# Rotary half-swap by VectorE's shuffle in place of products with a constant matrix

## The reference

```
parts = split(h @ w_in)                     # ten blocks of 1024 columns: b, c, xin, za, q, k, v, zb, ga, gb
q = apply_rope(heads(parts[4]), cos, sin)   # 16 heads of 64
k = apply_rope(heads(parts[5]), cos, sin)
v = heads(parts[6])
attn = neighbourhood_attention(q, k, v, k_ctx, v_ctx, rpb)
y = mixer_out(parts, attn, ...)

def rot_half_axial(u):                      # over the 64 features of a head
    u1, u2, u3, u4 = split(u, 4)            # four groups of 16
    return concatenate([-u2, u1, -u4, u3])
def apply_rope(u, cos, sin):
    return u * cos + rot_half_axial(u) * sin
```

## Time and profile before

| | us |
|---|---|
| median of 3 runs | 1343.25 |
| lowest and highest run | 1339.63, 1343.4 |
| profiled execution, its own time | 1342.57 |
| span of the profiled execution | 1340.4 |

### The profile page before, as it was taken

The page is one execution under the profiler, slowest core; times in us unless marked ns, Lnnn a source line. Parts: engine busy times, 40 slices in busy tenths (PEclk is TensorE's granted clock), DMA queues, the critical chain, the costliest instruction groups (busy, mean ns, idle before and its releaser), DMA issues.

```text
span 1340.4 us, 14669 instructions
## 1 busy us (share of the span) xinstructions
PE 1237.3 (92%) x6021; PEld 858.2 (64%) x6021; DVE 302.1 (23%) x652; ACT 207.4 (15%) x419; POOL 107.1 (8%) x117
## 2 busy tenths in 40 slices
PE   4999899999999989898989889889999999999997
PEld 4887788887853434434343324378888888876686
DVE  2035213543130111101110111121001004426511
ACT  1222452220110000000000000110000000025501
POOL 0015002510100000000000000000000000025300
PEclk9999899999989898898979898998999999999999
DMA  8879323333649999999999999952444444344300
GB/s 286 265 249 321 123 97 123 125 127 102 252 188 401 376 418 409 417 409 419 417 393 418 418 419 413 377 185 94 157 149 147 146 155 157 126 157 124 97 0 32
DMA packets 149737, 324.57 MB, mean 242 GB/s; under 512 B 8655, under 2 KB 111546, under 8 KB 133178
## 3 DMA queue, kind: packets, MB, share of 16 engines
q1 hardware_dynamic: 143818, 315.39, 63.0%
q0 software_dynamic: 1536, 4.20, 1.1%
q10 hardware_dynamic: 4336, 4.30, 1.0%
HBM read 321.77 MB, written 1.05 MB: 241 GB/s over the span
## 4 chain that ended last, share of the span: by engine, by line
PE 77%; DMA 8%; issue 7%; DVE 4%; ACT 2%; SPq 1%; POOL 1%; DVEq 0%; POOLq 0%; ACTq 0%
PE bank L551 31%; PE bank L817 14%; PE bank L554 13%; DMA ring<-in_w 7%; PE bank L837 5%; PE bank L794 3%; DVE X L1732 1%; PE bank L854 1%; PE bank L711 1%; PE bank L909 1%; DMA ring<-in_w_in 1%; PE bank L605 1%; PE bank L942 1%; PE bank L922 1%; ACT AR L1147 1%
## 5 line engine op out<-in xcount | busy, mean ns | idle before, releaser
L551 PE MATMUL bank<-HT,ring 128*128 128x256 f32 x1856 | 409.1, 382 | 4.3 <-DVE HT L1403 3.7
L551 PEld LDWEIGHTS bank<-HT,ring 128*128 128x128 f32 x1856 | 354.8, 192 | 56.4 <-DVE HT L1403 4.4
L817 PE MATMUL bank<-ring,AR 128*64 128x512 f32 x640 | 169.1, 593 | 3.9 <-DMA ring<-in_w 3.9
L554 PE MATMUL bank<-ring,HT 128*128 128x256 f32 (+1 forms) x576 | 129.1, 385 | 8.1 <-DMA ring<-in_w_in 6.9
L817 PEld LDWEIGHTS bank<-ring,AR 128*64 128x64 f32 x640 | 56.4, 137 | 112.9 <-issue 112.9
L554 PEld LDWEIGHTS bank<-ring,HT 128*128 128x128 f32 x576 | 110.3, 196 | 24.6 <-issue 8.2
L817 PE MATMUL bank<-AR 128*64 128x512 f32 x384 | 125.0, 663 | 0.1
L837 PE MATMUL bank<-ring,AR 128*64 128x512 f32 x384 | 87.7, 598 | 11.4 <-ACT AR L1147 11.4
L554 PE MATMUL bank<-ring,AR 128*128 128x256 f32 x328 | 74.5, 390 | 4.4 <-DVE AR L1850 1.5
L1720 DVE TENSOR_TENSOR AR<-AR,bank 128x256 f32<-128x256 f32 x32 | 13.5, 421 | 286.1 <-ACT AR L1140 286.1
L1267 POOL TENSOR_TENSOR SM<-SM 128x2 f32<-128x2 f32 (+3 forms) x9 | 12.3, 1368 | 787.7 <-DVE SM L1383 727.5
(11 more groups left out here) (307 smaller groups left out, 912.2 us busy)
## 6 DMA issues: line engine op xcount, KB each, us to landing
ring<-in_w SPq DMA_DIRECT2D x128, 1024.0 KB, 15.4
ring<-in_w_in SPq DMA_DIRECT2D x67, 1024.0 KB, 5.1
AR<-in_w SPq DMA_DIRECT2D x64, 1024.0 KB, 11.4
ring<-in_w_mod SPq DMA_DIRECT2D x12, 1024.0 KB, 6.0
ring<-in_w_out SPq DMA_DIRECT2D x4, 1024.0 KB, 6.0
ring<-in_w_ple_gate SPq DMA_DIRECT2D x4, 1024.0 KB, 9.7
ring<-in_w_out_conv SPq DMA_DIRECT2D x4, 1024.0 KB, 5.1
AR<-in_bias POOLq DMA_DIRECT2D x32, 128.0 KB, 2.4
```

What stands on the lines that cost most here:

```text
L551: mm = pe.matmul(bank[:, part * T:part * T + T], w[:, k, c0 + part * P:c0 + part * P + P], act[:, k, :], start=(k == 0), stop=(k == k_n - 1))
L554: mm = pe.matmul(bank[:, part * 256:part * 256 + n], act[:, k, part * P:part * P + P], w[:, k, c0:c0 + n], start=(k == 0), stop=(k == k_n ...
L817: mm = pe.matmul(bank[e * SLOT:e * SLOT + SLOT, :].rearrange("p (w n) -> p w n", w=2), XG[:, k, :], w, start=(k == 0), stop=(k == DK - 1))
```

## The change

The swap of the two groups of 16 partitions is done by one instruction of VectorE, `stream_shuffle`, which lets each partition of a group of 32 take the data of another of the same group. It reads `RAW` and writes into the destination of the rotated result. The minus sign of the rotation, which a shuffle can't give, is put into the table of sines. The multiplication by the sine table now reads and writes the destination in SBUF and no longer reads a PSUM bank. TensorE's eight products with `rot` fall away with their waits, and `rot` itself, 128 of the columns of `CST`. VectorE waits for ScalarE's copy in place of TensorE's product.

```
-            def rotate(m):
-                i = (of["q2"] + of["k2"])[m]
-                pe.wait_ge(S("emptied_act"), emptied[i][1])
-                if m >= 2:
-                    pe.wait_ge(S("roped"), m - 1)
-                pe.matmul(B[4 + m % 2][:, :], const("rot"), RAW[:, m % 2, :], start=True, stop=True)\
-                  .then_inc(S("rot_ps"), 1)
-            for m, i in enumerate(of["q2"] + of["k2"]):
-                product(i, HT)
-                if m:
-                    rotate(m - 1)
-            product(of["v2"][0], HT)
-            rotate(7)
-            for i in of["v2"][1:]:
-                product(i, HT)
+            products("q2", HT)
+            products("k2", HT)
+            products("v2", HT)
             pe.wait_ge(S("roped"), 8)
...
-                dve.wait_ge(S("rot_ps"), m + 1)
+                dve.wait_ge(S("emptied_act"), emptied[i][1])
                 d3 = dst.rearrange("p (a t) -> p a t", a=2)
-                V_.tensor_tensor(d3, B[4 + m % 2][:, :].rearrange("p (a t) -> p a t", a=2),
-                                 over(const("sinT").unsqueeze(1), 2, T), ALU.mult)
+                link(V_.stream_shuffle(dst, RAW[:, m % 2, :], [(lane + 16) % 32 for lane in range(32)]))
+                V_.tensor_tensor(d3, d3, over(const("sinT").unsqueeze(1), 2, T), ALU.mult)
...
-    put("sinT", np.sin(ang.astype(np.float64)))
+    put("sinT", np.sin(ang.astype(np.float64)) * np.where(i % 32 < 16, -1.0, 1.0)[:, None])
```

More of the change, by code:

```diff
@@ L60 @@
 CONST_COLS, _at = {}, 0
-for _name, _n in (("ident", 128), ("ustrict", 128), ("ones", 256), ("rot", 128), ("cosT", 256), ("sinT", 256),
+for _name, _n in (("ident", 128), ("ustrict", 128), ("ones", 256), ("cosT", 256), ("sinT", 256),
                   ("winmask", 256), ("invfreq", 16), ("iota_slot", 128), ("rev8", 8), ("pick2", 2), ("row0", 128), ("round_id", ROUNDS)):
@@ L79, in constants @@
     put("ones", 1.0)
[L81 to L87, removed]
     half = HD // 2
```

## The result

| | before | after |
|---|---|---|
| median, 14 runs each (us) | 1339.61 | 1331.34 |
| lowest and highest (us) | 1334.73, 1343.4 | 1323.78, 1335.54 |
| profiled execution (us) | 1342.57 | 1323.78 |
| its span (us) | 1340.4 | 1321.6 |

The ratio is 0.9929, with a 95% interval from 0.9907 to 0.9951: 9.5 us faster, between 6.6 and 12.5. It isn't the ratio of the two medians, which lie 8.3 us apart. One later execution of the kernel before took 3628.36 us, in the slow state, and is left out of every figure here. The kernel before came out at 1339.61 us over 14 runs; the three that the prediction had seen had a median of 1343.25.

A forecast was written before the change was run, and what follows sets the result against it. TensorE, busy without a gap in the queries and keys, was taken as the bound. Rotations (6.87 us) and shorter constant tile (0.2) sum to 7.07 us off the median 1343.25, giving 1336.2 us; range 1331.5 to 1340.

The forecast's parts named there:

- The place and the mechanism: Stage of queries and keys: eight rotations of 0.86 us are links of TensorE's chain; removing them takes off 6.87 us.
- The hidden work: VectorE, queries and keys: eight shuffles of 0.69 us, 5.8 us together with their waits, cost the path nothing.
- cover of a turn: VectorE, queries and keys: with the shuffle added, about 2 us stay idle in each turn of a 6.91 us product.
- The limit: Before the scores: each shuffle may take 5.7 us before TensorE waits for a rotated result.
- the banks' limit: Queries, keys and values: a product waits for the copy four products back, called looser than the limit of the scores.
- The constant tile: Start of the kernel: 64 KB less to load brings the first fill and product forward by 0.2 us, bounds 0 and 0.3.
- The biases' lead: GpSimd's first three biases, about 20 us ahead of the last copy of values, gain some 10 us on that lead.
- the last step of the sum: Whole kernel: 7.07 us taken off the median of 1343.25 us gives 1336.2 us.
- rival B: After the changed stage, perhaps at the scores: the gain is given back, 1343.1 us if all, 1339.7 if half; chance 0.12.

## Why the prediction was right or wrong

**The place and the mechanism held.** The rotations were links of the chain, and their removal shortened the stage by 6.86 us where 6.87 was forecast. Doubling them cost 6.87; VectorE's part without TensorE's gave nothing.

**The hidden work was hidden.** A shuffle takes 0.72 us where 0.69 was taken, plus the forecast gap and the short load of the permutation: 8 x 0.76 = 6.1 us of VectorE time in place of 5.8. The prediction's cover of a turn was right as well: 1.85 us of waiting behind a turn of queries, 2.30 behind one of keys. The rule of the Trainium skill, "VectorE: DVE Perf Modes", "The perf-mode tier table", that the shuffle has no faster program, agrees with the trace: 0.72 us is near the 0.69 of a one-pass row and far from 0.43. The eight took 5.8 us without their gaps, against the 5.5 that the prediction worked out by that rule. The limit, worked out as 5.7 us of shuffles per turn, was found between 5.3 and 7.6 us, and by the size of the wait at 5.7. The prediction called the banks' limit looser still; it is, and it was just reached at 7.65 us.

**The constant tile.** 0.2 us was taken out of 0 to 0.3; the issue moved by 0.1 us. The condition that the other input of the first product was ready at 19.23 us isn't fixed: in the first profile of the changed kernel it was ready at 20.6, and TensorE was then released by it. The term is too small to matter for the result.

**The biases' lead was mis-sized.** The prediction had it grow by some 10 us. The chunks of convolution were done 46.7 us behind the first copy, as worked out (1159 - 1112.4), where it was 58.2 before. But the scores themselves come 6.9 us earlier, which the prediction didn't take off, and the three biases now took 8.4 us behind the eighth chunk, where it was 6.1. Of the 2.3 us more, 1.88 are a wait for the transfer of a bias; the three additions themselves took 2.5 us in both, although the first ran beside VectorE's last turn. The timeline of the changed kernel:

```profile
1147.28 0.95 POOL L1336 MEMSET AR<- 128x1024 f32 x1 [253.76 <-DVE AR L1764]
...
1151.13 1.03 POOL L1342 TENSOR_TENSOR AR<-AR,CST 128x256 f32<-128x256 f32 x1 [0.58 <-DMA AR<-in_bias]
1151.61 1.10 DVE L1780 TENSOR_TENSOR AR<-AR 128x512 f32<-128x512 f32 x1
...
1154.04 0.73 POOL L1342 TENSOR_TENSOR AR<-AR,CST 128x256 f32<-128x256 f32 x1 [1.88 <-DMA AR<-in_bias]
...
1154.92 0.73 POOL L1342 TENSOR_TENSOR AR<-AR,CST 128x256 f32<-128x256 f32 x1
```

The third bias is ready at 1155.65 us, 21.6 us ahead of the first score, where it was 19.3 ahead before. It was cover in any case.

**What failed is the last step of the sum**, "off the median it is 1336.2 us", and with it the range from 1331.5 us. The gain of 7.07 us was taken from a median of three runs, 1343.25, as if that were the kernel's time. Two of the three lay at the upper end, which is chance: over 14, 25 and 33 runs in three comparisons the median was 1339.61, 1337.72 and 1337.97 us, and single runs went from 1329.81 to 1343.4 us, where the three had lain 3.8 us apart. Off 1339.61 the same sum gives 1332.5, and the changed kernel's median was 1331.34, 0.16 us under the range. The prediction had named the spread in its rival B and had not put it at the base. It also gave the lower end only one us for it (1339.63 - 7.2 - 1 is 1331.4, which it wrote as 1331.5). Of the 4.8 us between the likeliest time, 1336.2, and the measured 1331.34, 3.6 are the base and 1.2 the difference of the medians beyond 7.07.

**Is there more than 7.07 us?** The gain of 7.07 us is a ratio of 0.9947. It lies in both intervals measured for the changed kernel, 0.9907 to 0.9951 and 0.9940 to 0.9973. The stretch, the issue of the first fill and the tail account for 7 us in the profiles, and the rest of the difference of the two first profiles is found again, part by part, among profiles that have the first block unchanged. A real effect of 1 or 2 us on the first block can't be excluded by these intervals; nothing in the profiles points to one.

## What to carry to other kernels

Where one engine is busy without a gap, its links in the chain can be priced from the distance of two equal events on another engine, with and without the link; here that was exact to 0.01 us. Moved work is free as long as its sum over all turns up to the first real consumer fits, and as long as the buffers between, here `RAW` and the four banks, are emptied in time. That is more than what one turn has idle (5.7 us here, where a turn of queries had 2.6).

Set the forecast against how far runs of one kernel lie apart: with three runs, the base was wrong by 3.6 us or more, half of the gain. And before a difference of two profiles is explained, compare the stages that the change doesn't touch.

## What the runs showed of the hardware

A `stream_shuffle` of 128 x 512 float32 in SBUF takes 0.72 us, on all 128 partitions at once, and the load of its permutation 0.01 us each time. Ten in a row cost 0.76 to 0.77 us each from start to start.

After a wait of 14.9 us TensorE's clock stood at 0.57 in the first scores, near the lower of its two levels, and these eight matmuls took 3.46 us in place of 1.99 in the changed kernel, at a clock of 1.00. The cost was more than the wait.

The granted clock from 360 to 380 us of the same kernel was 0.66 in one execution and 0.91 in another, and the stages up to the first copy of queries took 1103.0 or 1112.4 us.
